# Feed-forward chunks 2 to 10 with the weights stationary: one 512-column and one 256-column product for each weight tile

## The reference

```python
for l in range(DEPTH):                                   # DEPTH = 2
    x = x + 0.5 * swiglu(rms_norm(x, ffn1_norm[l]), ffn1_w_gate[l], ffn1_w_up[l], ffn1_w_down[l])
    ...                                                  # attention, pooling, w_out
    x = x + 0.5 * swiglu(rms_norm(x, ffn2_norm[l]), ffn2_w_gate[l], ffn2_w_up[l], ffn2_w_down[l])

def swiglu(h, w_gate, w_up, w_down):
    return (jax.nn.silu(h @ w_gate) * (h @ w_up)) @ w_down
```

## Time and profile before

| | |
|---|---|
| median of 3 runs | 951.69 us (950.94 to 952.34) |
| the profiled execution's own time | 951.97 us |
| its span | 949.9 us |
| mean granted TensorE clock | 0.995 |
| PE busy | 931.3 us, 98% of the span |
| DVE busy | 551.5 us, 58% |
| ACT busy | 499.7 us, 53% |

### The profile page before, as it was taken

One profiled execution on the slowest core, in us unless ns is written; L12 is line 12 of the kernel. 1 busy time (PEld: TensorE's weight loads), 2 busy tenths in 40 slices (PEclk: granted clock), 3 DMA queues, 4 the chain that ended last, 5 costly groups with the idle time before them and its releaser, 6 DMA issues.

```text
span 949.9 us, 12733 instructions
## 1 busy us (share of the span) xinstructions
PE 931.3 (98%) x4299; PEld 760.5 (80%) x4299; DVE 551.5 (58%) x896; ACT 499.7 (53%) x821; POOL 44.6 (5%) x81
## 2 busy tenths in 40 slices
PE   8899999999999999999999999999999999999996
PEld 6688888877777888888888888888877888888885
DVE  4546465467755655645476545565686474554644
ACT  6545454456746554545465445454675374554542
POOL 1001010010001100100010000000100000000000
PEclk9999999999999999999999999999999999999999
DMA  7967868726235987675456656644534266465541
GB/s 240 251 202 165 230 175 288 257 90 232 104 110 143 273 183 234 158 222 180 133 189 210 220 182 246 213 157 164 175 139 146 74 237 209 172 210 188 168 142 45
DMA packets 123532, 174.66 MB, mean 184 GB/s; under 512 B 8384, under 2 KB 99696, under 8 KB 123248
## 3 DMA queue, kind: packets, MB, share of 16 engines
q1 hardware_dynamic: 117744, 165.70, 52.0%
q0 software_dynamic: 2848, 6.38, 5.5%
q10 hardware_dynamic: 2912, 2.22, 0.7%
HBM read 173.14 MB, written 4.19 MB: 187 GB/s over the span
## 4 chain that ended last, share of the span: by engine, by line
PE 92%; DVE 3%; ACT 2%; issue 2%; DMA 1%; SPq 0%; POOL 0%; POOLq 0%; DVEq 0%; ACTq 0%
PE ps L985 28%; PE ps L988 28%; PE ps L986 28%; PE ps L1082 2%; PE ps L995 1%; DVE w_lo L727 1%; PE ps L996 1%; PE ps L1195 1%; ACT xt_hi L487 1%; PE ps L1211 1%; PE ps L1223 1%; PE ps L1070 1%; DMA w_raw<-in_ffn_w_down_dram 1%; PE ps L1045 0%; DVE w_lo L718 0%
## 5 line engine op out<-in xcount | busy, mean ns | idle before, releaser
L985 PE MATMUL ps<-w_hi,xt_hi 128*128 128x512 f32 x856 | 342.1, 400 | 2.1 <-DVE xt_lo L741 1.1
L727 DVE SCALAR_TENSOR_TENSOR w_lo<-w_raw,gains,w_hi 128x512 fp32r<-128x512 f32 x416 | 285.1, 745 | 85.8 <-ACT w_hi L472 84.3
L986 PE MATMUL ps<-w_lo,xt_hi 128*128 128x512 f32 x856 | 334.3, 390 | 0.0
L988 PE MATMUL ps<-w_hi,xt_lo 128*128 128x512 f32 x856 | 329.5, 391 | 0.0
L472 ACT ACTIVATE w_hi<-w_raw,gains 128x512 fp32r<-128x512 f32 x408 | 260.7, 713 | 86.2 <-PE ps L988 81.5
L718 DVE TENSOR_TENSOR w_lo<-w_raw,w_hi 128x1024 fp32r<-128x1024 f32 x104 | 122.8, 1222 | 136.1 <-ACT w_hi L465 135.7
L985 PEld LDWEIGHTS ps<-w_hi,xt_hi 128*128 128x128 f32 x856 | 161.2, 188 | 40.3 <-issue 4.0
L988 PEld LDWEIGHTS ps<-w_hi,xt_lo 128*128 128x128 f32 x856 | 161.1, 188 | 34.8
L986 PEld LDWEIGHTS ps<-w_lo,xt_hi 128*128 128x128 f32 x856 | 161.4, 189 | 30.7
L465 ACT ACTIVATE w_hi<-w_raw 128x1024 fp32r<-128x1024 f32 x104 | 104.4, 1052 | 121.7 <-PE ps L988 114.4
L985 PE MATMUL ps<-w_hi,gt_hi 128*128 128x512 f32 x352 | 138.3, 393 | 3.3 <-DVE gt_lo L782 3.3
(11 more groups left out here) (84 smaller groups left out, 404.2 us busy)
## 6 DMA issues: line engine op xcount, KB each, us to landing
w_raw<-in_ffn_w_down_dram SPq DMA_DIRECT2D x88, 512.0 KB, 4.2
w_raw<-in_ffn_w_gate_dram SPq DMA_DIRECT2D x86, 512.0 KB, 4.0
w_raw<-in_ffn_w_up_dram SPq DMA_DIRECT2D x86, 512.0 KB, 5.1
w_raw<-in_w_in_dram SPq DMA_DIRECT2D x32, 512.0 KB, 4.8
w_raw<-in_w_out_dram SPq DMA_DIRECT2D x16, 512.0 KB, 5.3
bias_scratch<-in_rpb_dram POOLq DMA_DIRECT2D x32, 96.0 KB, 8.2
bias<-bias_scratch POOLq DMA_DIRECT2D x2, 1536.0 KB, 6.8
pool_m<-in_pool_matrix_dram ACTq DMA_DIRECT2D x1, 1024.0 KB, 9.3
```

The source lines that it names most:

```text
L727: nc.vector.scalar_tensor_tensor(w_lo[slot][:, part], w_raw[slot][:, part], g, w_hi[slot][:, part].bitcast(F32), ALU.mult, ALU.subtract).t ...
L985: nc.tensor.matmul(o, hi, wh, start=start, stop=False)
L986: nc.tensor.matmul(o, hi, wl, start=False, stop=False)
L988: last = nc.tensor.matmul(o, lo, wh, start=False, stop=bool(stop))
```

## The change

In each stage chunks 0 and 1 stay as they were (`TOKEN_MAJOR = 2`). For chunks 2 to 10 the operands of gate and up change places: a 128x128 tile of weights is stationary and the activations move. For each weight tile `w_hi` meets `x_both`, 256 columns of high and 256 of low activations side by side (512 columns), and `w_lo` meets `x_h`, the 256 high columns, and is added to the first half of the bank. Each result (hidden columns on partitions, tokens along the bank) lies in two halves: gate in banks 0 and 1, up in banks 6 and 7. ACT copies the low half of a pair of banks to SBUF and DVE adds the high half to it (`sum_gate` for gate; the first step of `gate_t` for up). No transposes are needed for these chunks, and the split of `gated` reads SBUF.

Since the tokens now lie along the free dimension, the activations must be normalised before: `broadcast_rstd` turns rstd into a row with two products, DVE multiplies the transposed residual (which now stays in the four accumulator banks until then) by gain and row (`normalise_xt`, 8 instructions), ACT and DVE split the result into `xn`. The units of gate and up are then split without gains, in pieces of 1024. The transposes of the residual go to banks 2 to 5 instead of 6 and 7.

```diff
             def chunk(layer, ff, i, first):
...
+                pe.wait_ge(normed_t_ready, 2 * ff_no(layer, ff) + 2)
+                all_down(layer, ff, i - 1, first)
...
+            def gate_up_t(layer, ff, i, a, free_gate=None, free_up=None):
+
+                slot = ff["g"][a]
+                number = unit_no(layer, ff["stage"], slot, i)
+                for m, free in ((0, free_gate), (1, free_up)):
+                    if free:
+                        pe.wait_ge(*free)
+                    for j in range(2):
+                        bank = GU_BANKS[m][j]
+                        for k in range(4):
+                            if (m, j) == (0, 0):
+                                wait_split(slot, number, k + 1)
+                            c = k * BANK + m * FC + j * P
+                            w_h, w_l = w_hi[slot][:, c:c + P], w_lo[slot][:, c:c + P]
+                            x_h = xn[:, 4 * a + k, 0, :]
+                            x_both = xn[:, 4 * a + k, :, :].rearrange("p o q -> p (o q)")
+                            if (a, k) != (0, 0):
+                                nc.tensor.matmul(ps[:, bank, 0:SEQ], w_l, x_h, start=False, stop=False)
+                            last = nc.tensor.matmul(ps[:, bank, :], w_h, x_both,
+                                                    start=(a, k) == (0, 0), stop=(a, k) == (1, 3))
+                            if (a, k) == (0, 0):
+                                nc.tensor.matmul(ps[:, bank, 0:SEQ], w_l, x_h, start=False, stop=False)
...
+                broadcast_rstd(layer, ff)
                 chunk(layer, ff, 1, True)
...
+                transpose_gated(layer, ff, 1)
+                pe.wait_ge(xn_lo_ready, 2 * ff_no(layer, ff) + 2)
+                gate_up_t(layer, ff, 2, 0, free_up=(gt_lo_ready, gt_no(layer, ff, 1) + 1))
+                all_down(layer, ff, 1)
+                gate_up_t(layer, ff, 2, 1)
+                with pe.Fori(TOKEN_MAJOR + 1, LAST) as i:
+                    done = transposed_no(layer, ff, i)
+                    gate_up_t(layer, ff, i, 0, (gate_summed, done), (up_summed, up_summed_no(layer, ff, i)))
+                    all_down(layer, ff, i - 1)
+                    gate_up_t(layer, ff, i, 1)
+                gate_up_t(layer, ff, LAST, 0, (gate_summed, transposed_no(layer, ff, LAST)),
+                          (up_summed, up_summed_no(layer, ff, LAST)))
+                gate_up_t(layer, ff, LAST, 1)
...
+            def silu_t_of(layer, ff, i):
+                act.wait_ge(gate_ready, transposed_no(layer, ff, i) + 1)
+                nc.scalar.activation(silu[:, :, :], ps[:, 0:2, SEQ:], ACT.Copy
+                                     ).then_inc(gate_low_stored, 1)
+                act.wait_ge(gate_summed, transposed_no(layer, ff, i) + 1)
+                nc.scalar.activation(silu[:, :, :], silu[:, :, :], ACT.Silu
+                                     ).then_inc(silu_t_ready, 1)
+                act.wait_ge(up_ready, transposed_no(layer, ff, i) + 1)
+                act.wait_ge(gt_lo_ready, gt_no(layer, ff, i))
+                nc.scalar.activation(gated[:, :, :], ps[:, 6:8, SEQ:], ACT.Copy
+                                     ).then_inc(up_low_stored, 1)
...
+            def sum_gate(layer, ff, i):
+
+                dve.wait_ge(gate_low_stored, transposed_no(layer, ff, i) + 1)
+                nc.vector.tensor_tensor(silu[:, :, :], ps[:, 0:2, 0:SEQ], silu[:, :, :], ALU.add
+                                        ).then_inc(gate_summed, 1)
+
+            def gate_t(layer, ff, i, number, part):
+
+                dve.wait_ge(up_low_stored, transposed_no(layer, ff, i) + 1)
+                nc.vector.tensor_tensor(gated[:, :, part], ps[:, 6:8, part], gated[:, :, part],
+                                        ALU.add).then_inc(up_summed, 1)
+                dve.wait_ge(silu_t_ready, transposed_no(layer, ff, i) + 1)
+                dve.wait_ge(up_summed, number + 1)
+                nc.vector.scalar_tensor_tensor(gated[:, :, part], gated[:, :, part], 0.5,
+                                               silu[:, :, part], ALU.mult, ALU.mult
+                                               ).then_inc(gated_t_ready, 1)
...
+                with dve.Fori(TOKEN_MAJOR, LAST) as i:
+                    unit(layer, ff, g0, i + 1)
+                    unit(layer, ff, ff["d"], i)
+                    sum_gate(layer, ff, i)
+                    gate_t(layer, ff, i, up_summed_no(layer, ff, i), slice(0, SEQ))
+                    unit(layer, ff, g1, i + 1, halves=(0,))
+                    split_gated_lo(layer, ff, i)
+                    unit(layer, ff, g1, i + 1, halves=(1,))
```

More of the change, by code:

```diff
@@ L194, in trunk @@
         gated_ready = [sem(f"gated_ready{t}") for t in range(TT)]
+        gate_low_stored = sem("gate_low_stored")
+        gate_summed = sem("gate_summed")
+        up_low_stored = sem("up_low_stored")
+        up_summed = sem("up_summed")
+        gate_ready = sem("gate_ready")
+        up_ready = sem("up_ready")
+        silu_t_ready = sem("silu_t_ready")
+        gated_t_ready = sem("gated_t_ready")
+        rstd_row_ready = sem("rstd_row_ready")
+        rstd_row_stored = sem("rstd_row_stored")
+        normed_t_ready = sem("normed_t_ready")
+        xn_hi_ready = sem("xn_hi_ready")
+        xn_lo_ready = sem("xn_lo_ready")
         gt_ready = sem("gt_ready")
@@ L793, in unit @@
-            def unit(layer, ff, slot, k, gains_from=None):
+            def sum_gate(layer, ff, i):
[11 more added lines that the diff above has]
+                                               ).then_inc(gated_t_ready, 1)
@@ new lines, in normalise_xt @@
+            def normalise_xt(layer, ff):
+                dve.wait_ge(rstd_row_stored, ff_no(layer, ff) + 1)
+                for k in range(KT):
+                    h, c = k // 4, (k % 4) * P
+                    done = nc.vector.scalar_tensor_tensor(
+                        normed_t(k).rearrange("p (t q) -> p t q", t=TT),
+                        ps[:, 2 + h:6 + h:2, c:c + P], gains[:, ff["stage"], layer, k:k + 1],
+                        rstd_row[:, :].rearrange("p (t q) -> p t q", t=TT), ALU.mult, ALU.mult)
+                    if k % 4 == 3:
+                        done.then_inc(normed_t_ready, 1)
@@ L794, in unit, with split_xn_lo @@
+            def split_xn_lo(layer, ff, h):
+                dve.wait_ge(xn_hi_ready, 2 * ff_no(layer, ff) + h + 1)
+                nc.vector.tensor_tensor(xn[:, 4 * h:4 * h + 4, 1, :],
+                                        normed[:, h, :].rearrange("p (k q) -> p k q", k=4),
+                                        xn[:, 4 * h:4 * h + 4, 0, :].bitcast(F32), ALU.subtract).then_inc(xn_lo_ready, 1)
+            def unit(layer, ff, slot, k, gains_from=None, halves=(0, 1)):
                 split_lo(slot, unit_no(layer, ff["stage"], slot, k),
-                         gains_of=None if gains_from is None else (ff["stage"], layer, gains_from))
+                         gains_of=None if gains_from is None else (ff["stage"], layer, gains_from),
+                         halves=halves)
@@ L935, in store_gains @@
                     gains[:, first:last, :, :].rearrange("p j l k -> p (j l k)"),
-                    ps[:, 4 - n, first * DEPTH * KT:last * DEPTH * KT]).then_inc(gains_stored, 1)
+                    ps[:, 5 + n, first * DEPTH * KT:last * DEPTH * KT]).then_inc(gains_stored, 1)
             store_gains(1, 0, 1)
@@ L1084, in transpose_gated, with broadcast_rstd @@
                 last.then_inc(gt_ready, 1)
-            def transpose_last_gated(layer, ff, t):
-                pe.wait_ge(gated_ready[t], chunk_no(layer, ff, LAST) + 1)
-                for k in range(2):
-                    last = nc.tensor.transpose(ps[:, 7 - t, k * P:(k + 1) * P],
-                                               gated[:, t, k * P:(k + 1) * P], ident[:, :])
-                last.then_inc(gt_ready, 1)
+            def broadcast_rstd(layer, ff):
+                for t in range(TT):
+                    pe.wait_ge(rstd_ready[t], layer * STAGES + (ff["stage"] + 1))
+                    last = nc.tensor.matmul(ps[:, 7, t * P:(t + 1) * P],
+                                            rstd[:, t, :].to_broadcast([P, P]), ident[:, :],
+                                            start=True, stop=True)
+                last.then_inc(rstd_row_ready, 1)
@@ L1129, in chunk, with all_down @@
                         transpose_gated(layer, ff, i - 1)
-                n = unit_no(layer, ff["stage"], d, i - 1)
+                pe.wait_ge(normed_t_ready, 2 * ff_no(layer, ff) + 2)
+                all_down(layer, ff, i - 1, first)
+            def all_down(layer, ff, i, first=False):
+                n = unit_no(layer, ff["stage"], ff["d"], i)
                 for t in range(TT):
                     for k in range(2):
-                        last = down(layer, ff, i - 1, t, k, d, n, t == 0, start=first and k == 0)
+                        last = down(layer, ff, i, t, k, ff["d"], n, t == 0, start=first and k == 0)
```

175 lines of the change are left out of this document (109 added, 66 removed).

## The result

| | before | the change |
|---|---|---|
| median, same chip, in turn | 952.02 us (4 runs) | 962.04 us (961.63 to 962.79, 4 runs) |
| span of the profiled execution | 949.9 us | 960.1 us |
| mean granted TensorE clock | 0.995 | 0.992 |

What follows compares the result with a forecast made beforehand. PE was taken as the bound; -17.5 (transposes) + 3.1 (pairs) + 1.6 (rstd row) + 4.8 (bank 7) + 2.4 (last chunk) = -5.6 us against 951.97, giving 946.4, stated as a median of 946.2 us; range 938.5 to 954.0.

Steps and rivals of the forecast that it cites:

- So only what changes PE's own row of work, or makes PE wait, can move the time: Whole kernel: PE is busy 931.3 of 949.9 us, DVE and ACT a little over half, so PE is the bound.
- Removed, -17.5: Chunks 2 to 10 of each stage: dropped transposes save 4.4 us a stage, -17.5 us in four stages.
- I take the row, 0.116: Gate and up pairs: short product steps by 0.116 us, as in plain float32 pooling, long by 0.2267; +3.1 us.
- the first rival: Gate and up: 0.0133 us extra belongs to each product; float32 pooling's two passes would hide it; 950.7 us, chance 0.23.
- a few hundredths behind it: Old loop: small remainder of the 0.49 us transpose break, after the transposes and the late next product.
- The slow rival: Gate and up: weight load not wholly hidden under a short product, step 0.130 us; 962.3 us, chance 0.16.
- Row of rstd, +1.6: Stage head on PE: four steps of about 0.11 us plus restart, 0.53 us in three stages, hidden in the first.
- Bank 7, +4.8: Up of chunk 2 waits for `gt_lo` of chunk 1: 1.2 us a stage with restart, bounds 0 and 2.
- begins at E + 0.26, because it needs the slot that down has just left: Bank 7 wait: ACT's high part of the next down unit starts 0.26 us after chunk 0's down ends (E).
- Each load starts when DVE leaves the slot: Inside the loop: down load starts at T - 1.7, while ACT wants its data at T + 10.9.
- Last chunk, +2.4: Before the last chunk's down PE waits 0.5 us and restarts with 0.1; four stages, bounds 0 and 1 each.
- Inside the loop, no wait: Between chunks the gated result is ready at T + 4.3, against 5.5 us of pairs on PE: no wait.

Runs made afterwards that it cites:

- e7: Changed kernel with chunk 1's `gt` split ahead of its down unit and, in three stages, DVE's down unit ahead of `normed`: 957.15 us, ratio 1.0046.
- e6: Changed kernel with 16 long (512-column), then 16 short (256-column) products in turn in chunks 3 to 10: 958.57 us, ratio 1.0064 to the kernel before.
- e4: Changed kernel with DVE splitting chunk 0's down unit ahead of the eight `normed` instructions: 960.69 us, ratio 1.0085 to the kernel before.
- e10: Changed kernel with GpSimd's bias gathers three chunks later: 958.00 us, ratio 1.0062 to the kernel before.
- e2: Changed kernel without the `w_lo` products in chunks 2 to 10, so part of the sum is missing: 904.31 us (one run).

## Why the prediction was wrong

By its own steps:

- **"So only what changes PE's own row of work, or makes PE wait, can move the time"** held. DVE at 61% and ACT at 53% never became the bound.
- **Removed, -17.5:** held. The period of the changed kernel has no room for transposes (11.26 + 5.44 = 16.70), and the spans add up with it: e7's FF1 stage in the second layer is 187.51 us, as before, where -4.4 for transposes meets 9 x 0.38 = +3.4 for the pairs, +0.45 for the row and +0.4 for the tail.
- **"I take the row, 0.116", +3.1: the step that failed in size.** The term took 0.2267 + 0.116 = 0.343 us for a pair, and a pair takes 0.352: measured, the term is +13.7. In the mix the short step was 0.118, near enough; the sum kept 0.2267 for the long product behind it, and that was 0.234. With the pairs apart (e6), the short one is 0.120: the first rival was right that 0.0133 us belongs to every product, and wrong in that it also kept 0.2267 for all the long ones. The settled steps, 0.2267 + 0.120, are worth 0.13 of the 0.29 us that a chunk missed; the rest, 6 us in 36 chunks, comes only with the mix. Why a mix costs more is not shown.
- **Why the row misled:** it is of another number type. In plain float32 256 columns step by 0.217 us, which is 2 x 0.1067 + 0.003, and 136 columns by 0.116, which is 2 x 0.0567 + 0.003; this factor of 2 is all that the rows show of the "two passes" in the first rival. So these products carry 0.003 us over their columns where float32r, in rows 3 already, carries 0.0133. A hint of the mix stood in the prediction too: "a few hundredths behind it", after the transposes, looks like the same effect and was not asked of short products.
- The slow rival (0.130 a short step, 962.3 us) had nearly the right time by luck: no short product at full clock stepped by 0.130.
- **The range:** its upper end, 954.0, was said to hold the 0.120 step with waits at their upper bound. That sum is 946.2 + 4.6 + 3.2 + 1.6 = 955.6: 7.7 instead of 3.1 for the pairs, 4 x 2 instead of 4.8 at bank 7, 4 x 1 instead of 2.4 at the last chunk.
- The Trainium skill ("TensorE: Matmul & The Clock Gate", "Wait — 56ns, not 53.3ns?") puts some 2.5 ns on top of a product's columns. No run here agrees for this number type: it is 13.3 ns at 512 columns and at 256.
- **Row of rstd, +1.6:** 1.4, and hidden in the first stage, as said. The four steps take 0.36 us, as the transposes do, and not 4 x 0.11.
- **Bank 7, +4.8: the second step that failed, in one stage.** Right in three stages (1.3 us each, 1.2 forecast). In the fourth the wait was 3.6 us with a lower clock behind it, some 6.1 us in all. The failed step is that ACT's high part "begins at E + 0.26, because it needs the slot that down has just left". It needs the data too. "Each load starts when DVE leaves the slot" was said for the loop alone; in the head, where the eight new instructions hold the slot 3.2 us longer, it was not followed on to the landing. e4 and e10 show both causes. The upper bound of 2 us a stage did not hold it.
- **Last chunk, +2.4:** 1.6; the wait is there, 0.3 us instead of 0.5.
- **Inside the loop, no wait:** held in this kernel. The period was off by the pairs alone.

Of the miss of 16 us the pairs are 10.6 and the seam with the clock 5.2; the smaller terms were 1.0 us too high together. What is left, 1 us, is the balance of the 0.9 us that the terms say too much, the 0.4 us ahead of the first stage, and the mixing stage of the second layer, 90.30 us against 88.74, where ACT waits for data once:

```profile
696.11 1.34 ACT L515 ACTIVATE w_hi<-w_raw,gains 128x512 fp32r<-128x512 f32 x2 [1.56 <-DMA w_raw<-in_w_in_dram]
```

In the profiles of the other runs that stage lasts from 88.7 to 92.1 us, without a pattern that an edit explains. Its cause stays open, and differences of one or two microseconds between two profiled spans carry this scatter.

## What to carry to other kernels

Price a product by the step it has among its neighbours: a shape that is cheap by itself can slow the next one, and where one form must be mixed with another, long runs of each are cheaper than turns. When an instruction is put ahead of the last reader of a load buffer, follow the buffer on to the load's issue, its landing under the traffic of that moment, and the engine that wants it; a wait that is small by the engines' rows can be several microseconds by the load, and the clock can fall behind it, as it did here. Look also at how much earlier than needed the load landed in the kernel before: here it was 0.4 us. In an engine's program, splitting a unit whose data may be late should not stand ahead of short work that the bound engine waits for, unless the bound engine wants the unit first. The first and last turns of a loop may need an order of their own for this reason.

## What the runs showed of the hardware that had not been expected

- **Steps of TensorE with float32r operands settle over several products.** In a long row 512 columns step by 0.227 us (e2) and 256 by 0.120 (e6). In turns they are 0.234 and 0.118, 0.352 a pair against 0.347 for the two settled ones; in groups of four 0.233 and 0.118. In e6 the long products behind a short row lose 0.03 us in all before they have settled, and 0.05 us are lost in a row of long ones at the start of a chunk, with no short product near. Why is not shown.
- **A load of two 512 KB parts took about twice as long while gathers of 96 KB ran on GpSimd's queue:** a median of 7.1 us from issue to landing in the changed kernel and 7.4 in the kernel before, 3.8 with the gathers moved (e10).
- **An idle time of 3.45 us was followed by the 1.2 GHz level** (granted 0.50 in the next 4 us). Behind the idle time of 1.06 us at the seam of FF1 in the second layer the granted clock stayed at 1.00.
